# Prompt attention of a decoder step: VectorE takes unit u+1's maxima before it scales unit u

## What is computed

```python
s = einsum(q, k) * d ** -0.5            # d is 64 or 128
s = where(mask, s, NEG_INF)
m = max(s, axis=-1)
e = where(mask, exp(s - m), 0.0)
p = e / max(sum(e), 1e-30)              # NSA: times the branch's gate
o = einsum(p, v)
```

## Time and profile before

| | |
|---|---|
| median of 3 runs | 2241.76 us (2237.62 to 2242.25) |
| time of the profiled execution | 2242.91 us |
| its span | 2241.1 us |
| busy: TensorE, VectorE, ScalarE, GpSimd | 90%, 43%, 34%, 3% of the span |
| DMA traffic, mean | 236 GB/s |
| mean granted clock of TensorE | 0.953 of full |
| prompt attention | about 590 to 785 us of the span |
| of it the NSA units with the adaLN steps | up to 754 us |
| of it the dilated units | 754 to 785 us |

### The profile page before, as it was taken

How to read it: one execution, slowest core, us unless ns; L and a number is a source line. 1 busy time by engine, 2 the same in 40 slices (tenths; PEclk the granted TensorE clock), 3 DMA queues, 4 the chain that set the end, 5 groups by cost and what they waited for, 6 DMA issues and landing times.

```text
span 2241.1 us, 36633 instructions
## 1 busy us (share of the span) xinstructions
PE 2020.3 (90%) x15733; PEld 1847.4 (82%) x15733; DVE 971.7 (43%) x1693; ACT 762.2 (34%) x1200; POOL 65.9 (3%) x116
## 2 busy tenths in 40 slices
PE   4996999998799768788999999799999999999978
PEld 3675999998545535577999998799999999999967
DVE  2445465542344433124444474544443444544425
ACT  1345333343244411014333343433333333533312
POOL 0000000000000001000000000000000000000010
PEclk9998999999799978898999999899999999999988
DMA  7893798997599456646556565477777777577782
GB/s 254 353 354 113 226 287 266 292 292 247 222 421 420 195 184 243 233 139 207 172 173 200 173 194 185 138 248 255 243 246 251 238 258 250 167 256 250 241 290 85
DMA packets 354920, 530.00 MB, mean 236 GB/s; under 512 B 19473, under 2 KB 329017, under 8 KB 337385
## 3 DMA queue, kind: packets, MB, share of 16 engines
q1 hardware_dynamic: 324706, 369.34, 50.3%
q0 software_dynamic: 6400, 142.51, 16.3%
q10 hardware_dynamic: 23712, 16.69, 2.5%
HBM read 521.77 MB, written 98.91 MB: 277 GB/s over the span
## 4 chain that ended last, share of the span: by engine, by line
PE 83%; DMA 9%; DVE 5%; ACT 2%; ACTq 1%; issue 1%; SPq 0%; DVEq 0%
PE bank L1047 17%; PE bank L1049 16%; PE bank L1048 16%; PE bank L787 5%; PE bank L788 5%; PE bank L789 4%; DMA piece<-in_w_ada 4%; PE bank L686 3%; PE bank L723 3%; DMA piece<-in_w_down 2%; PE bank L942 1%; PE bank L972 1%; PE bank L712 1%; PE bank L1004 1%; PE bank L882 1%; PE bank L932 1%
## 5 line engine op out<-in xcount | busy, mean ns | idle before, releaser
L1047 PE MATMUL bank<-piece,piece 128*128 128x264 f32 x3072 | 881.4, 287 | 52.3 <-DVE piece L1891 26.3
L1048 PE MATMUL bank<-piece,piece 128*128 128x264 f32 x3072 | 877.5, 286 | 0.0
L1049 PE MATMUL bank<-piece,piece 128*128 128x264 f32 x3072 | 877.2, 286 | 0.0
L1896 DVE TENSOR_TENSOR piece<-piece,piece 128x2048 fp32r<-128x2048 f32 (+2 forms) x216 | 440.7, 2053 | 543.0 <-ACT piece L1435 543.0
L1047 PEld LDWEIGHTS bank<-piece,piece 128*128 128x128 f32 x3072 | 582.9, 190 | 54.1 <-issue 22.4
L1048 PEld LDWEIGHTS bank<-piece,piece 128*128 128x128 f32 x3072 | 582.4, 190 | 0.5
L1049 PEld LDWEIGHTS bank<-piece,piece 128*128 128x128 f32 x3072 | 582.7, 190 | 0.0
L1435 ACT CAST piece<-piece 128x2048 fp32r<-128x2048 f32 (+2 forms) x216 | 368.8, 1715 | 601.0 <-PE bank L1049 520.4
L787 PE MATMUL bank<-piece,piece 128*128 128x264 f32 (+1 forms) x816 | 240.2, 294 | 10.9 <-DVE piece L1660 10.9
L789 PE MATMUL bank<-piece,piece 128*128 128x264 f32 (+1 forms) x816 | 234.0, 287 | 0.0
L788 PE MATMUL bank<-piece,piece 128*128 128x264 f32 (+1 forms) x816 | 234.0, 287 | 0.0
(11 more groups left out here) (292 smaller groups left out, 1579.5 us busy)
## 6 DMA issues: line engine op xcount, KB each, us to landing
piece<-in_w_ada SPq DMA_DIRECT2D x48, 2048.0 KB, 12.7
out_s_dil<-in_cache_dil_kv POOLq DMA_DIRECT2D x64, 1023.5 KB, 6.3
piece<-in_w_in SPq DMA_DIRECT2D x50, 1024.0 KB, 8.2
piece<-in_w_gate SPq DMA_DIRECT2D x22, 2048.0 KB, 8.1
piece<-in_w_up SPq DMA_DIRECT2D x22, 2048.0 KB, 8.1
piece<-in_w_down SPq DMA_DIRECT2D x32, 1408.0 KB, 7.4
piece<-in_w_in SPq DMA_DIRECT2D x16, 2048.0 KB, 8.2
piece<-in_w_out SPq DMA_DIRECT2D x8, 2048.0 KB, 8.3
```

The source lines that it names most:

```text
L1047: mm(out, w_high[:, k, :], half_tile(x_high[k]), start=(start and k == first_tile), stop=False)
L1048: mm(out, w_high[:, k, :], half_tile(x_low[k]), start=False, stop=False)
L1049: last = mm(out, w_low[:, k, :], half_tile(x_high[k]), start=False, stop=(stop and k == len(x_high) - 1))
L1896: v.tensor_tensor(half_chunk(a, k_tiles, f, CW), raw, half_chunk(buffer, k_tiles).bitcast(F32), ALU.subtract)\
```

## The change

Taking the maxima and scaling become two functions, and VectorE's loop puts them in another order: maxima of unit 0, then for each u the maxima of unit u+1 and the scaling of unit u. The scratch of the maxima gets a second place, `small[:, 36:39]` beside `small[:, 32:35]`. The instructions themselves, and the programs of TensorE, ScalarE, SyncE and GpSimd, stay as they are.

```diff
-        for u in range(NU):
+        def unit(u):
             kind, qt, h = UNITS[u]
-            W = P * (qt + 1)
             c = 8 * (u % 2)
-            mx, nm, den = small[:, 32:35], small[:, c:c + 3], small[:, 16 + c:19 + c]
-            e = E[:, u % 2, :]
+            return kind, qt, h, P * (qt + 1), small[:, c:c + 3], small[:, 16 + c:19 + c], E[:, u % 2, :]
+
+        def maxima(u):
+            kind, qt, h, W, nm, den, e = unit(u)
+            mx = small[:, 32 + 4 * (u % 2):35 + 4 * (u % 2)]
             if u == 0:
                 dve.wait_ge(*act_.at("kvc", "p"))
             if u >= 2:
...
                 v.tensor_scalar(nm, mx, -SC_N, None, ALU.mult).then_inc(*dve_.mark("nm", u))
-                dve.wait_ge(*act_.at("e", u))
...
                 v.tensor_scalar(nm[:, 0:1], mx[:, 0:1], -SC_D, None, ALU.mult).then_inc(*dve_.mark("nm", u))
-                dve.wait_ge(*act_.at("e", u))
+
+        def normalised(u):
+            kind, qt, h, W, nm, den, e = unit(u)
+            dve.wait_ge(*act_.at("e", u))
+            if kind == "n":
...
+            else:
                 link(v.reciprocal(den[:, 0:1], den[:, 0:1]))
                 v.tensor_scalar(e[:, 0:3 * W], e[:, 0:3 * W], den[:, 0:1], None, ALU.mult).then_inc(*dve_.mark("p", u))
+
+        maxima(0)
+        for u in range(NU):
+            if u + 1 < NU:
+                maxima(u + 1)
+            normalised(u)
             if u >= ADA_STEPS + 2 and u % ADA_STEPS == 2 and u <= NA - NA1 + 2:
                 ada_mod(ADA_FIRST + u // ADA_STEPS - 1)
```

More of the change, by code:

```diff
@@ L1742, in _ @@
                 v.tensor_scalar(nm, mx, -SC_N, None, ALU.mult).then_inc(*dve_.mark("nm", u))
-                dve.wait_ge(*act_.at("e", u))
+            else:
+                mask = const("dilmask")[:, 0:3 * P] if qt == 0 else const("dilmask")[:, 3 * P:9 * P]
+                v.tensor_tensor_reduce(e[:, 0:2 * W], bank[0][:, 0:2 * W], mask[:, 0:2 * W], 1.0, -3e38, ALU.add, ALU.max,
+                                       mx[:, 0:1]).then_inc(*dve_.mark())
+                v.tensor_tensor_reduce(e[:, 2 * W:3 * W], bank[1][:, 0:W], mask[:, 2 * W:3 * W], 1.0, -3e38, ALU.add, ALU.max,
+                                       mx[:, 1:2]).then_inc(*dve_.mark("max", u))
+                dve.wait_ge(*dve_.last())
+                link(v.tensor_tensor(mx[:, 0:1], mx[:, 0:1], mx[:, 1:2], ALU.max))
+                v.tensor_scalar(nm[:, 0:1], mx[:, 0:1], -SC_D, None, ALU.mult).then_inc(*dve_.mark("nm", u))
+        def normalised(u):
+            kind, qt, h, W, nm, den, e = unit(u)
+            dve.wait_ge(*act_.at("e", u))
+            if kind == "n":
                 link(v.tensor_tensor_reduce(e[:, 2 * W:2 * W + NBP], e[:, 2 * W:2 * W + NBP],
```

## The result

| | before | after |
|---|---|---|
| median | 2239.69 us (4 runs, 2231.24 to 2242.25) | 2278.88 us (4 runs, 2274.99 to 2280.70) |
| profiled execution | 2242.91 us | 2280.70 us |
| its span | 2241.1 us | 2278.9 us |
| TensorE's mean clock | 0.953 | 0.946 |
| scores of unit 32 begin | 754.07 us | 764.04 us |

The ratio is 1.0167, with a 95% interval of 1.0140 to 1.0194: some 37 to 39 us slower. The forecast was slower by 21 us, 2253 to 2272. The direction is right and the size is not: the measured loss lies outside the range. The lines of VectorE have moved: the maxima are L1739 (before L1737) and L1747 (L1759), the NSA scaling ends with L1770 (L1755), the dilated one with L1774 (L1768).

A forecast was written before the change was run, and what follows sets the result against it. adaLN weight loads were taken to bound the NSA units at 5.0 us each. With +7.5 us by unit 32's scores and +13.8 in the dilated units, the stage ends 21.2 us later: 2241.76 + 21.2 = 2263 us, range 2253 to 2272.

The forecast's parts named there:

- What bounds, and what the change does: Prompt attention: adaLN loads pace NSA units at 5.0 us; after the change, VectorE and TensorE wait for each other by turns.
- NSA turns: Units 0 to 31: 4.575 us of TensorE work plus a 0.865 us stall makes 5.44 us a turn.
- the covering step: NSA turns: TensorE's adaLN step of 1.85 us, which runs while VectorE takes maxima and scales.
- the path: NSA turns: VectorE's start, maxima and scaling, from the end of scores until probs may start; 2.65 or 2.78 us.
- The start of the stage: NSA part up to the scores of unit 32: they start at 761.5 instead of 754.07 us, +7.5 us.
- Dilated turns: Units 32 to 39: waits and work sum to 44.6 us against 30.8, +13.8 us.
- After the stage: Behind the prompt attention: later work hangs on its end, so the +21.2 us shift goes through to the end.
- the third rival: Dilated units: TensorE's clock falls and its work doubles, +21 us, giving 2284 us; chance 0.08.
- The first rival: NSA units: loads hide the stall, pace stays 5.0 us, only the dilated part is paid, 2255.6 us; chance 0.08.
- The faster one: Dilated units: look-ahead finds its scores ready and 4.9 us of TensorE's waits go, giving 2236.9 us; chance 0.04.
- The range: Whole kernel: 2253 to 2272 us, reaching past the first rival; the clock, the faster case and tails lie outside.

The follow-up runs named there:

- the dilated part alone: Kernel before, with VectorE's look-ahead only between dilated units (32 to 39) and NSA units in the old order; ratio 1.0124 (1.0084 to 1.0165).
- its part alone: Kernel before, with VectorE's look-ahead only between NSA units (0 to 31) and dilated units in the old order; ratio 1.0045 (1.0022 to 1.0067).
- the run with two filling matmuls: Changed kernel plus two unused 256-column matmuls (0.87 us) behind the scores in each dilated turn; 2266.89 us, one execution.
- without cover: Changed kernel with the adaLN step moved behind pv, to the end of TensorE's turn; 2430.7 us, one execution.

## Why the prediction was wrong, step by step

- *What bounds, and what the change does*: right. VectorE's look-ahead asks for scores that TensorE issues only just before it needs the scaling. The runs show it: with the scores a turn earlier the loss of 37 us is gone.
- *NSA turns*: 5.42 us against 5.44, the loads no longer the bound, landing in 8.1 us. Without the covering step TensorE waits 2.6 us in the mean; the path was put at 2.65 to 2.78.
- *The start of the stage*: 764.04 instead of 761.5. Of these 2.5 us, 1.1 came into the stage with it (VectorE's L1721 ends at 593.7 instead of 592.6), and 1.4 is one adaLN step at half clock (3.29 us, by the timeline) that was not in the sum.
- *Dilated turns*: the sum of waits and work was 44.6 us, and with the clock held at full it measures 45.7.
- *After the stage*: right. The stage ends 38.4 us later and the span is 37.8 us longer.
- *The step that failed* is the clock in that stretch: "By that rule the time would be that of the third rival; by the rows alone, the forecast", and the 0.08 given to the rival. The sum took every duration at full clock because a window of the kernel before showed 1.00. But that window had waits of 1.2 us in the mean in every second turn (4.9 us in four, the longest 1.9); the forecast itself put 2.0 to 2.2 us in every turn. The row said nothing of such a pattern, and I let it outweigh a rule that does. The fall took place in all three runs with these waits and nothing to fill them (the changed kernel twice, the dilated part alone), for 13.5 to 15.3 us of the 38.4 by which the stage ends later. With the smaller value the account closes: 21.2 forecast, 2.5 from the start, 45.7 - 44.6 = 1.1 from the waits and work, 13.5 from the clock, 38.3 in all. The third rival's price of 21 us was for half clock throughout; the clock was between its levels, at 0.69 in the mean.
- So the rule of the Trainium skill ("TensorE: Matmul & The Clock Gate", "A second HAM failure mode: psum-queue depth-cycling"), that frequent short stops can make the clock swing, agrees with these traces (mean clock 0.69 and 0.80 with the stops, 1.00 with them filled).
- *The first rival* (loads hide the NSA part) is out: its part alone costs 10 us. *The faster one* is out too: VectorE's waits for the scores became longer, and even with the scores a turn earlier the time is the same within 0.2 to 0.4%.
- *The range* had no room for the one rival whose condition the forecast's own numbers met. With 13.5 us for the clock beside the 21.2, the forecast would have been about 2276.

What stays open: how long or how dense the stops must be for the clock to fall, since waits of 0.84 us beside long steps left it at full, and in the run with two filling matmuls it fell once. It is open too why the clock swung less with the dilated part alone (0.81 over the stretch) than with both parts (0.69). The runs with two filling matmuls and without cover were executed once each.

## What to carry to other kernels

A look-ahead must be made on the engine that produces as well as on the one that consumes: before moving work on one engine, ask when the other issues what the moved instruction waits for, and what it needs right after it. Whoever forecasts new stops of TensorE in every turn should put the work around them at both clocks; a window at full clock vouches only for its own pattern of stops. And a transfer that starts one step early can delay the one that the path waits for.

## What had not been expected of the hardware

- Stops of about 2 us in dilated turns that would last 4.8 us at full clock let TensorE's clock swing between 1.2 and 2.4 GHz: means of 0.69 and 0.80 over 56 and 50 us. Filling these stops with 0.87 us of unused matmuls in each turn brought the mean back to 0.96, with 1.73 us to 1.00. In the NSA turns without cover, with stops of 2.6 us in turns of 10.3, it was 0.67 over 144 us.
- With two page gathers of 2 MB beside it, the last load of 2 MB took 18.9 us; with the gathers later it took 13.8, and TensorE's last wait for weights fell from 6.3 to 1.2 us.
